# Second block: a fourth high-part buffer, tile 5 split before the first rotation, and a new order on ScalarE in the second attention

## Chip, cores and metric

The kernel runs on one core of a Trainium2 chip. The metric is the device time of one execution in microseconds; the median of three runs of the kernel before is 1157.89 us (1157.75 to 1158.03).

## What is computed

One sequence of 256 tokens with 1024 features passes through a first block of two layers (retention, forgetting attention and an RWKV-7 recurrence, gated and merged, then a gated feed-forward net) and a second block of two layers, with which this change deals. Cut to what matters, a layer of the second block is

```
h = rmsnorm(x, norm_g)                 # [256, 1024]
z = h @ w_in                           # 3328 columns: q,k,v,gate of branches a, b, c, d
q_a,k_a = axial_rope(rmsnorm(q_a)), axial_rope(rmsnorm(k_a)); o_a = softmax(q_a k_a^T / 8) v_a
q_b,k_b = rope(q_b), rope(k_b);        o_b = softmax with window and a sink logit
o_c = neighbourhood attention with a relative bias
o_d = (softmax(q1 k1^T) - lam * softmax(q2 k2^T)) v_d, rmsnorm
x = x + concat(o_a*silu(g_a), o_b*silu(g_b), o_c*silu(g_c), o_d*silu(g_d)) @ w_out
```

## The kernel before

Every large product is done in three passes of a float32 kind that TensorE takes fast: a weight tile is split into a high part (ScalarE, a copy that rounds) and a low part (VectorE, the tile minus the high part), and so is the activation.

In the second block the input projection goes over 13 groups of 256 columns. A group's weights are a tile of 1 MB, 128 x 2048. SyncE loads tile n into ring slot n % 4 once TensorE has finished group n - 3. ScalarE writes the high part (`in_split2` in its program, line 1373), VectorE the low part in place of the tile (`in_split2` in its program, line 1827). The high parts have three buffers in turn (`high2[l][n % 3]`), so ScalarE's helper `next_high(l, g)` waits for TensorE's group g before it splits tile g + 3. Tile 5 therefore waited for group 2. TensorE does a group in two units ("pieces", 12 matmuls of 512 columns each, line 669): pieces 2n and 2n + 1 belong to tile n, and a group's first piece waits for its tile's low part. Groups 0 to 11 come in pairs, which are copied out of PSUM by ScalarE together (`pair_out`, line 1652).

Every engine works its program in the written order; there is no planner. The order around the change is this, in each of the two layers.

TensorE: pieces 0 to 9 (tiles 0 to 4), with the norm's sum of squares in between; then the turn (transposes, line 1262) of q and k of branch a, which waits for the rotation; then piece 10, which waits for tile 5; then four attentions (`attend(n)`). In an attention the scores of heads 0 and 1 come first, a piece, the turn of the gate (`y_transposes`, line 754), a piece, then the wait for the gate's copy, `weigh(0)` (transposes of the probabilities, line 803), the scores of heads 2 and 3, `weigh(1)`, a piece, the values of a pair (line 826), `weigh(2)`, and so on. `weigh(h)` waits for the normalised probabilities of head h (VectorE, line 1897) and for the copy of the turned probabilities of head h - 1 (ScalarE's `copy`, line 1451).

VectorE: low parts of tiles 2, 3 and 4, the head sums of branch a, small products for lambda, then the wait for GpSimd's inverse roots (`b_rs`), the rotation (lines 2406, 2409, 1857, 1865, 1867), low parts of tiles 5 and 6, the gate product `(tanh + 1) * z` (line 2378), and the first attention. In an attention it makes for each head a mask addition (line 1909; none in the first) and a maximum, after each pair of heads the normalisation (`normed`), and splits of tiles at set places.

ScalarE: copy-outs, high parts, the tanh of a gate (`gate_sigmoid`, line 1670), and in the attentions the exponentials (`exps(n)`, line 1442), the copy of the turned gate (`gate_copy`, line 1428) and the copies of turned probabilities.

SyncE: the tile loads in order, line 551; between tile 4 and tile 5 its queue holds a wait for the norm's sum and the load of a small vector, and the load of the relative bias stands behind tile 7. GpSimd: the inverse roots (line 2488) and, when the relative bias has landed, two additions of it to the mask (line 2526).

Of the kernel before, what the change touches and what calls it, by code (L numbers as in the profile page):

```python
# [17 lines left out]
F32 = mybir.dt.float32  # L18
F32R = mybir.dt.float32r
ALU = mybir.AluOpType  # L20
ACT = mybir.ActivationFunctionType
AX = mybir.AxisListType

P = 128
D = 1024
KT = D // P
# [149 lines left out]
def build(nc, x_in, w_in, w_fox, lora_w, p_all, w_out, w_gate_up, w_down, cols, vec1, mu, w_in2, w_out2,  # L176
          vec2, rpb, tables, out):
    with ExitStack() as ctx:
        def sb(name, shape):
            return ctx.enter_context(nc.sbuf_tensor(name, shape, F32))  # L180
# [12 lines left out]
        ring = sb("ring", [P, RING, 2048])  # L193
        vec = sb("vec", [P, N_VEC1])
        yT_at = -(-nc.sbuf_base // 32) * 32
        yT = sb("yT", [P, 3, 2, S])
        lora = sb("lora", [P, 2, W4])
        w_f = sb("w_f", [P, KT, NH])
        w_f32 = sb("w_f32", [P, KT, 32])
        gain = sb("gain", [P, FINAL + 1, KT])  # L200
# [15 lines left out]
        def v2(n):  # L216
            return vec[:, VEC2[n][0]:VEC2[n][0] + VEC2[n][1]]
# [30 lines left out]
        in_high = [nc.alloc_sbuf_tensor_at(f"in_high{i}", [P, KT, 256], F32R, offset=ring_at + 8192 * (4 + i)) for i in range(2)]  # L248
        in_third = nc.alloc_sbuf_tensor_at("in_third", [P, KT, 256], F32R, offset=scratch_at + 4 * 2560)
        high2 = [(*in_high, in_third), (in_high[0], in_third, in_high[1])]  # L250
        in_low = [nc.alloc_sbuf_tensor_at(f"in_low{i}", [P, KT, 256], F32R, offset=ring_at + 8192 * i) for i in range(4)]

        wo_high = [nc.alloc_sbuf_tensor_at(f"out_high{q}", [P, 2, D], F32R, offset=o)
# [373 lines left out]
        def _(pe):  # L627
# [17 lines left out]

            def split_operands(n, l=None):

                return (in_high[n % 2] if l is None else high2[l][n % 3]), in_low[n % 4]

            def token_major(w, out, t):  # L650

# [693 lines left out]
        def _(act):  # L1345
# [24 lines left out]
            def in_split2(l, n):  # L1370

                act.wait_ge(*ring_in2[n % 4].after(l, n // 4 + 1))
                f(high2[l][n % 3][:], ring[:, n % 4, :].rearrange("p (k n) -> p k n", k=KT), ACT.Copy).then_inc(in_hi2.sem, 1)

            def in_split(l, n, slots, done):

# [271 lines left out]
            def pair_out(l, g):  # L1648

                act.wait_ge(*b_full.after(l, g + 2))  # L1650
                for t in range(NT):
                    last = f(z2[:, t, g * 256:(g + 2) * 256], bank[(g + t) % 4][:], ACT.Copy, scale=rstd_x[:, t:t + 1])
                last.then_inc(b_out.sem, 2)

            def next_high(l, g):

                act.wait_ge(*b_full.after(l, g + 1))
                in_split2(l, g + 3)
# [8 lines left out]
            def gate_sigmoid(l, c0):  # L1667

                e = b_eg_t.rearrange("p (t c) -> p t c", t=NT)
                f(e, z2[:, :, c0:c0 + W4], ACT.Tanh, scale=0.5).then_inc(b_eg.sem, 1)  # L1670

            qs = HD ** -0.5

            for l in range(DEPTH):
                in_split2(l, 2)
                next_high(l, 0)
                next_high(l, 1)
                sums(2 * DEPTH + l)
                act.wait_ge(*norms.root.after(2 * DEPTH + l, 1))
                pair_out(l, 0)  # L1680
                next_high(l, 2)
                act.wait_ge(*b_lam.after(l, 1))
                f(st[:, 200:202], st[:, 200:202], ACT.Exp).then_inc(b_lame.sem, 1)
                next_high(l, 3)
                pair_out(l, 2)
                next_high(l, 4)
                act.wait_ge(*b_out.after(l, 4))
                gate_sigmoid(l, 512)
                turned(l, 0, 256, qs)

                def gate_copy(n):
                    if n:
                        act.wait_ge(*b_mT.after(l, n))
                    y_copy(l, n, b_mtp, gT, bank[6], b_gT, 0.5)

                exps, copy = attention(l, att, 0, 0, 1, lambda n: bank[4 + n % 2])
                exps(0)
                exps(1)
                gate_copy(0)
                pair_out(l, 4)  # L1700
                next_high(l, 5)
                copy(0)
                copy(1)
                exps(2)
                exps(3)
                copy(2)
                next_high(l, 6)
                copy(3)
                turned(l, 2, 256, qs)
                pair_out(l, 6)  # L1710
                act.wait_ge(*b_out.after(l, 6))
                gate_sigmoid(l, 1280)

                exps, copy = attention(l, att, 4, 4, 1, lambda n: a_s[:, n % 2, :], sink=True)
                exps(0)
                exps(1)
                gate_copy(1)
                next_high(l, 7)
                copy(0)
                copy(1)  # L1720
                exps(2)
                exps(3)
                copy(2)
                next_high(l, 8)
                copy(3)
                turned(l, 4, 512, qs)
                pair_out(l, 8)
                next_high(l, 9)
                act.wait_ge(*b_out.after(l, 10))
                gate_sigmoid(l, 2304)  # L1730

                exps, copy = attention(l, att, 8, 8, 1, lambda n: a_s[:, n % 2, :])
                exps(0)
                exps(1)
                gate_copy(2)
                copy(0)
                copy(1)
                exps(2)
                exps(3)
                pair_out(l, 10)  # L1740
                copy(2)
                copy(3)
                turned(l, 6, 256, 32 ** -0.5)
                act.wait_ge(*b_full.after(l, G2))
                scaled(z2[:, :, (G2 - 1) * 256:G2 * 256], bank[(G2 - 1) % 4][:].rearrange("p (t c) -> p t c", t=2), rstd_x)\
                    .then_inc(b_out.sem, 1)
                fetch_x(l, x_saved2, x_back2)

                exps, copy = attention(l, att, 12, 12, 2, lambda n: bank[4 + n % 2])
                exps(0)  # L1750
                exps(1)
                exps(2)
                exps(3)
                copy(0)
                if l + 1 < DEPTH:
                    in_split2(l + 1, 0)
                exps(4)
                exps(5)
                copy(1)
                gate_sigmoid(l, 3072)  # L1760
                if l + 1 < DEPTH:
                    in_split2(l + 1, 1)
                exps(6)
                exps(7)
                copy(2)
                copy(3)
                act.wait_ge(*att.y.after(l, 4))
                f(b_t2, bank[7][:], ACT.Square).then_inc(b_lame.sem, 1)
                y_copy(l, 3, b_mtp, mixT[3], bank[7], b_mT, 0.5)
                if l + 1 < DEPTH:  # L1770
                    norm(2 * DEPTH + l + 1, fresh, x_saved2)
                else:

                    f(small[:, 9:10], eps6, ACT.Sqrt)
                    for j in range(4):
                        act.wait_ge(*x_ready.after(FINAL, j + 1))
                        f(squares[:, 2 * j:2 * j + 2, :], fresh[:, 2 * j:2 * j + 2, :], ACT.Square).then_inc(norms.sq.sem, 1)
                    act.wait_ge(*norms.summed.after(FINAL, 1))
                    f(root[:], bank[4][:, 0:S], ACT.Sqrt, scale=1.0 / D, bias=eps6).then_inc(norms.root.sem, 1)
# [3 lines left out]
        def _(dve):  # L1783
# [40 lines left out]
            def in_split2(l, n):  # L1824

                dve.wait_ge(*in_hi2.after(l, n + 1))
                tt(in_low[n % 4][:], ring[:, n % 4, :].rearrange("p (k n) -> p k n", k=KT), high2[l][n % 3][:].bitcast(F32),  # L1827
                   ALU.subtract).then_inc(in_lo2.sem, 1)

            def half_split2(l, n, half):  # L1830

                dve.wait_ge(*in_hi2.after(l, n + 1))
                k = slice(4 * half, 4 * half + 4)
                last = tt(in_low[n % 4][:, k, :], ring[:, n % 4, :].rearrange("p (k n) -> p k n", k=KT)[:, k, :],
                          high2[l][n % 3][:, k, :].bitcast(F32), ALU.subtract)
                if half:
                    last.then_inc(in_lo2.sem, 1)

# [527 lines left out]
            for l in range(DEPTH):  # L2366
# [35 lines left out]
                fence()  # L2402
                red(st[:, 200:202], st[:, 260:324].rearrange("p (a c) -> p a c", a=2), AX.X, ALU.add).then_inc(b_lam.sem, 1)
                ts(st[:, 330:394], v2("subln"), v2("one_less"), None, ALU.mult)
                dve.wait_ge(*b_rs.after(l, 1))
                tt(q_rot, qk6(0), put(st[:, 112:124].rearrange("p (t h) -> p t h", t=NT), 3, HD), ALU.mult)
                fence()
# [1 line left out]
                    tt(q_rot[:, :, h0:h1, :], q_rot[:, :, h0:h1, :], put(put(v2(n), 1, h1 - h0), 1, NT), ALU.mult)  # L2409
                fence()  # L2410
                rope(q_rot, q_t1, q_t2, q_rot, 6, "axial", 16).then_inc(b_rot.sem, 1)
                for n in range(5, 7):
                    in_split2(l, n)
                gate_ready(l, 1, 512)
                attention(l, att, 0, 4, 1, None, splits={1: lambda l: in_split2(l, 7)})

# [191 lines left out]
```

## Time and profile before

| | us |
|---|---|
| median of three runs | 1157.89 |
| the profiled execution's own time | 1157.58 |
| its span | 1155.5 |
| TensorE busy | 1126.9 |
| VectorE busy | 767.5 |
| ScalarE busy | 524.1 |

The second block covers the span from about 863 us on; layer 1 of it begins at about 1003. TensorE's granted clock is full (1.00) in all of it but the last microseconds. Times in rows are from the span's start. Engines are named PE (TensorE), PEld (its weight loads), DVE (VectorE), ACT (ScalarE), POOL (GpSimd), SPq (SyncE's DMA queue). A row of a timeline has the start, the duration, the engine, the line, the operation, what it writes and reads, the count of merged instructions, and in brackets how long the engine stood idle before it and which instruction ended that.

### The profile page before, as it was taken

To read this page: it belongs to the slowest core of one execution; us is meant where nothing else is said; L and a number is where in the kernel's file an instruction comes from. 1 tells how busy PE (TensorE), PEld (TensorE's weight loads), DVE (VectorE), ACT (ScalarE), POOL (GpSimd) and SP (SyncE) were. 2 spreads that over 40 slices of the span, in tenths; PEclk is the share of its full clock that TensorE was granted. 3 is DMA by queue.
4 is the path that set the end of the run, shared out by engine and by line. 5 is a ranking of instruction groups with operands and counts; after the bars stand their busy time and mean duration, and the time that the engine had idled before them with its cause. 6 is when DMAs were issued, how large, how long until landed. Compare 5 with 4: busy or idle time off the path is not lost. (4 is left out here: it accounts for less than half of the span.)

```text
span 1155.5 us, 21951 instructions
## 1 busy us (share of the span) xinstructions
PE 1126.9 (98%) x9400; PEld 1013.9 (88%) x9400; DVE 767.5 (66%) x1104; ACT 524.1 (45%) x734; POOL 65.7 (6%) x51
## 2 busy tenths in 40 slices
PE   5999999999999999999999999999999999999997
PEld 4789989899999998798998999999997768877785
DVE  5587765867565665787665965556667685677744
ACT  5355443534333344465334443333355565446642
POOL 1002000100000000011001000000001100030000
PEclk9999999999999999999999999999999999999999
DMA  9543335445354355443335355534436234353320
GB/s 358 222 163 110 116 109 188 176 164 224 159 218 187 144 199 187 146 146 111 111 111 220 109 219 219 216 140 189 181 141 229 109 111 182 115 218 134 116 79 37
DMA packets 27610, 188.16 MB, mean 163 GB/s; under 512 B 3472, under 2 KB 4368, under 8 KB 5776
## 3 DMA queue, kind: packets, MB, share of 16 engines
q1 hardware_dynamic: 25952, 175.89, 40.7%
q10 hardware_dynamic: 1440, 8.55, 1.9%
q0 software_dynamic: 144, 2.66, 0.6%
q8 instruction: 56, 0.92, 0.3%
q14 instruction: 18, 0.15, 0.0%
HBM read 181.84 MB, written 5.24 MB: 162 GB/s over the span
## 5 line engine op out<-in xcount | busy, mean ns | idle before, releaser
L669 PE MATMUL bank<-in_low,h_high 128*128 128x512 f32 x352 | 138.3, 393 | 0.0
L669 PE MATMUL bank<-in_high,h_high 128*128 128x512 f32 x288 | 117.5, 408 | 12.5 <-DVE in_low L1977 11.8
L1089 PE MATMUL bank<-h_high,gate_split 128*128 128x256 f32 x704 | 128.8, 280 | 0.2
L1089 PE MATMUL bank<-h_high,up_split 128*128 128x256 f32 x704 | 128.6, 280 | 0.0
L1105 PE MATMUL bank<-act_split,down_split 128*128 128x256 f32 x960 | 118.4, 283 | 0.0
L1105 PEld LDWEIGHTS bank<-act_split,down_split 128*128 128x128 f32 x960 | 116.6, 192 | 0.0
L694 PE MATMUL bank<-h_high,in_high 128*128 128x256 f32 x384 | 115.8, 302 | 0.5 <-DVE in_low L1851 0.5
L1378 ACT ACTIVATE in_high<-ring 128x2048 fp32r<-128x2048 f32 x47 | 89.6, 1910 | 54.9 <-PE bank L669 53.6
L669 PE MATMUL bank<-in_high,x_low 128*128 128x512 f32 x288 | 113.1, 393 | 0.0
L1089 PEld LDWEIGHTS bank<-h_high,gate_split 128*128 128x128 f32 x704 | 109.9, 189 | 0.9 <-DVE h_low L1793 0.6
L1089 PEld LDWEIGHTS bank<-h_high,up_split 128*128 128x128 f32 x704 | 109.8, 189 | 0.0
L694 PE MATMUL bank<-x_low,in_high 128*128 128x256 f32 x384 | 108.4, 282 | 0.0
L694 PE MATMUL bank<-h_high,in_low 128*128 128x256 f32 x384 | 108.3, 282 | 0.0
L1851 DVE TENSOR_TENSOR in_low<-ring,in_high 128x2048 fp32r<-128x2048 f32 x35 | 79.9, 2289 | 35.4 <-ACT in_high L1378 35.4
L1089 PE MATMUL bank<-h_low,up_split 128*128 128x256 f32 x352 | 99.2, 282 | 0.0
L1089 PE MATMUL bank<-h_low,gate_split 128*128 128x256 f32 x352 | 99.1, 282 | 0.0
L1609 ACT ACTIVATE gate_split<-ring 128x2048 fp32r<-128x2048 f32 x24 | 46.0, 1916 | 73.2 <-PE bank L1089 71.5
L2290 DVE TENSOR_TENSOR down_split<-ring,down_split 128x2048 fp32r<-128x2048 f32 x20 | 45.9, 2292 | 50.0 <-ACT down_split L1609 50.0
L669 PEld LDWEIGHTS bank<-in_low,h_high 128*128 128x128 f32 x352 | 66.7, 189 | 13.2 <-issue 0.5
L694 PEld LDWEIGHTS bank<-h_high,in_high 128*128 128x128 f32 x384 | 73.1, 190 | 5.7 <-issue 1.4
L669 PEld LDWEIGHTS bank<-in_high,h_high 128*128 128x128 f32 x288 | 54.5, 189 | 26.3 <-issue 14.3
L694 PEld LDWEIGHTS bank<-x_low,in_high 128*128 128x128 f32 x384 | 73.4, 191 | 0.1
(348 smaller groups left out, 2385.2 us busy)
## 6 DMA issues: line engine op xcount, KB each, us to landing
ring<-w_in_dram SPq DMA_DIRECT2D x71, 1024.0 KB, 4.9
ring<-w_gate_up_dram SPq DMA_DIRECT2D x44, 1024.0 KB, 8.3
ring<-w_down_dram SPq DMA_DIRECT2D x22, 1024.0 KB, 4.8
ring<-w_out_dram SPq DMA_DIRECT2D x16, 1024.0 KB, 6.5
ring<-p_all_dram SPq DMA_DIRECT2D x6, 1024.0 KB, 4.8
x_kept<-scratch ACTq DMA_DIRECT2D x4, 1024.0 KB, 3.9
x<-x_kept ACTq DMA_DIRECT2D x4, 1024.0 KB, 8.4
table<-tables_dram POOLq DMA_DIRECT2D x1, 2594.0 KB, 11.9
```

Source lines behind the costliest of these rows:

```text
L669: last = mm(bank[(n - n % 2 + t) % 4][:], a, b, start=c == 0 and i == 0, stop=c == KT - 1 and i == 2)
L694: last = mm(bank[g % 4][:, half * 256:(half + 1) * 256], a, b, start=k == 0 and i == 0, stop=k == KT - 1 and i == 2)
L1089: last = mm(bank[2 * half + part][:, f * S:(f + 1) * S], a, b, start=k == 0 and i == 0, stop=k == KT - 1 and i == 2)
L1105: last = mm(bank[4 + m // 2][:, m % 2 * S:(m % 2 + 1) * S], a, b, start=False, stop=end and m % 2 == 1 and k == 1 and i == 2)
L1378: f(in_high[n % 2][:], ring[:, n % 4, :].rearrange("p (k n) -> p k n", k=KT), ACT.Copy).then_inc(done.sem, 1)
L1609: f(w_split[part if pair is None else pair][:, 0, :], ring[:, 3 * half + part, :], ACT.Copy).then_inc(w_hi[part].sem, 1)
L1851: tt(in_low[n % 4][:], ring[:, n % 4, :].rearrange("p (k n) -> p k n", k=KT), in_high[n % 2][:].bitcast(F32), ALU.subtract).then_inc(low.s ...
L2290: tt(w[:, 1, :], ring[:, 3 * half + part, :], w[:, 0, :].bitcast(F32), ALU.subtract)\
```

## The change

A tensor of 512 columns is laid behind `lora`, so that there is room for a fourth high-part buffer, over parts of `yT` and `lora` that the second block does not use and that new tensor. Tile 5 of each layer goes into it. ScalarE splits tile 5 without a wait for group 2. VectorE makes the low part of tile 5 before the wait for the inverse roots and the rotation, and no longer behind it. In front of the second attention ScalarE does the second gate's tanh ahead of the copy-out of groups 6 and 7; in it, the gate's copy comes between the first two exponentials, and the split of tile 10 comes behind the first two copies of turned probabilities.

```
         lora = sb("lora", [P, 2, W4])
+        sb("after_lora", [P, 512])
...
+        in_fourth = nc.alloc_sbuf_tensor_at("in_fourth", [P, KT, 256], F32R, offset=yT_at + 4 * 512)
+
+        def high_of(l, n):
+            return in_fourth if n == 5 else high2[l][n % 3]
...
-                return (in_high[n % 2] if l is None else high2[l][n % 3]), in_low[n % 4]
+                return (in_high[n % 2] if l is None else high_of(l, n)), in_low[n % 4]
...
                 pair_out(l, 0)
-                next_high(l, 2)
+                in_split2(l, 5)
                 act.wait_ge(*b_lam.after(l, 1))
...
                 turned(l, 2, 256, qs)
-                pair_out(l, 6)
                 act.wait_ge(*b_out.after(l, 6))
                 gate_sigmoid(l, 1280)
+                pair_out(l, 6)
 
                 exps, copy = attention(l, att, 4, 4, 1, lambda n: a_s[:, n % 2, :], sink=True)
                 exps(0)
+                gate_copy(1)
                 exps(1)
-                gate_copy(1)
-                next_high(l, 7)
                 copy(0)
                 copy(1)
+                next_high(l, 7)
                 exps(2)
...
                 ts(st[:, 330:394], v2("subln"), v2("one_less"), None, ALU.mult)
+                in_split2(l, 5)
                 dve.wait_ge(*b_rs.after(l, 1))
...
                 rope(q_rot, q_t1, q_t2, q_rot, 6, "axial", 16).then_inc(b_rot.sem, 1)
-                for n in range(5, 7):
-                    in_split2(l, n)
+                in_split2(l, 6)
                 gate_ready(l, 1, 512)
```

The other hunks write `high_of(l, n)` for `high2[l][n % 3]` in the splits of both engines.

## Rows read from the trace of the kernel before

**Rows 1.** The page's part 1: busy time, share of the span, instructions.
```profile
PE 1126.9 (98%) x9400; PEld 1013.9 (88%) x9400; DVE 767.5 (66%) x1104; ACT 524.1 (45%) x734; POOL 65.7 (6%) x51
```

**Rows 2.** TensorE's waits, 860 to 1156 us: total, times, longest.
```profile
PE bank L669 <- DVE in_low L1827: 1.6, 2, 0.9
PE bank L803 <- ACT scratch L1451: 1.3, 2, 0.7
PE bank L803 <- ACT scratch L1428: 0.9, 2, 0.5
...
```

**Rows 3.** Timeline of TensorE at the first turn, both layers.
```profile
891.15 0.82 PE L1262 MATMUL bank<-table,scratch 128*128 128x128 f32 x6
892.89 0.50 PE L669 MATMUL bank<-in_third,h_high 128*128 128x512 f32 x1 [0.92 <-DVE in_low L1827]
...
1032.15 0.82 PE L1262 MATMUL bank<-table,scratch 128*128 128x128 f32 x6
1033.67 0.49 PE L669 MATMUL bank<-in_high,h_high 128*128 128x512 f32 x1 [0.71 <-DVE in_low L1827]
```

**Rows 4.** Timeline of ScalarE: the high part of tile 5, both layers.
```profile
884.81 1.92 ACT L1373 ACTIVATE in_third<-ring 128x2048 fp32r<-128x2048 f32 x1 [4.24 <-DMA ring<-w_in_dram]
...
1025.53 1.92 ACT L1373 ACTIVATE in_high<-ring 128x2048 fp32r<-128x2048 f32 x1 [4.18 <-DMA ring<-w_in_dram]
```

**Rows 5.** Timeline of SyncE's queue: loads of tiles 5 to 7, layer 0.
```profile
877.89 8.34 SPq L551 DMA_DIRECT2D ring<-w_in_dram  x3
```

**Rows 6.** Timeline of VectorE: the first rotation and what follows, both layers.
```profile
885.43 0.96 DVE L2406 TENSOR_TENSOR scratch<-arena,small 128x768 f32<-128x768 f32 x1 [2.25 <-POOL small L2488]
...
889.68 0.96 DVE L1867 TENSOR_TENSOR scratch<-scratch 128x768 f32<-128x768 f32 x1
890.55 2.29 DVE L1827 TENSOR_TENSOR in_low<-ring,in_third 128x2048 fp32r<-128x2048 f32 x1
892.76 2.28 DVE L1827 TENSOR_TENSOR in_low<-ring,in_high 128x2048 fp32r<-128x2048 f32 x1
894.96 2.87 DVE L2378 SCALAR_TENSOR_TENSOR scratch<-scratch,arena 128x512 f32<-128x512 f32 x1
...
1026.21 0.96 DVE L2406 TENSOR_TENSOR scratch<-arena,small 128x768 f32<-128x768 f32 x1 [2.25 <-POOL small L2488]
```

**Rows 7.** Timeline of GpSimd: the first bias addition, both layers.
```profile
893.15 4.13 POOL L2526 TENSOR_TENSOR scratch<-scratch,table 128x1024 f32<-128x1024 f32 x1 [7.75 <-DMA scratch<-rpb_dram]
...
1033.95 4.11 POOL L2526 TENSOR_TENSOR scratch<-scratch,table 128x1024 f32<-128x1024 f32 x1 [7.78 <-DMA scratch<-rpb_dram]
```

**Rows 8.** Timeline of VectorE in the second attention, layer 0.
```profile
919.46 0.69 DVE L2378 SCALAR_TENSOR_TENSOR scratch<-scratch,arena 128x512 f32<-128x512 f32 x1 [4.08 <-ACT scratch L1670]
...
931.37 0.15 DVE L1891 TENSOR_TENSOR stats<-stats,small 128x2 f32<-128x2 f32 x1
```

**Rows 9.** Timeline of TensorE in the second attention, layer 0.
```profile
917.53 1.13 PE L787 MATMUL bank<-scratch 64*128 64x256 f32 x8
...
921.50 0.60 PE L754 MATMUL bank<-table,scratch 128*128 128x128 f32 x4
...
925.34 0.66 PE L803 MATMUL bank<-table,scratch 128*128 128x128 f32 x4 [0.45 <-ACT scratch L1428]
...
927.71 0.63 PE L803 MATMUL bank<-table,scratch 128*128 128x128 f32 x4 [0.65 <-ACT scratch L1451]
...
932.51 0.66 PE L803 MATMUL bank<-table,scratch 128*128 128x128 f32 x4 [0.27 <-DVE scratch L1897]
```

**Rows 10.** Timeline of ScalarE in the second attention, layer 0.
```profile
921.86 0.51 ACT L1442 ACTIVATE scratch<-scratch,stats 128x256 f32<-128x256 f32 x1 [2.43 <-DVE stats L1923]
...
924.71 0.57 ACT L1428 ACTIVATE scratch<-bank 128x512 f32<-128x512 f32 x1
925.19 1.90 ACT L1373 ACTIVATE in_high<-ring 128x2048 fp32r<-128x2048 f32 x1
```

**Rows 11.** Windows: busy us of each engine, PEclk (granted clock), DMA share, GB/s.
```profile
1152.00:1156.00 4.00, 0.00 (x0) 0.00 (x0) 0.52 (x1) 0.00 (x0) 0.00 (x0) 0.50 0.64 255
```

More of the change, by code:

```diff
@@ L197, in build @@
         lora = sb("lora", [P, 2, W4])
+        sb("after_lora", [P, 512])
         w_f = sb("w_f", [P, KT, NH])
@@ L250, in build, with high_of @@
         high2 = [(*in_high, in_third), (in_high[0], in_third, in_high[1])]
+        in_fourth = nc.alloc_sbuf_tensor_at("in_fourth", [P, KT, 256], F32R, offset=yT_at + 4 * 512)
+        def high_of(l, n):
+            return in_fourth if n == 5 else high2[l][n % 3]
         in_low = [nc.alloc_sbuf_tensor_at(f"in_low{i}", [P, KT, 256], F32R, offset=ring_at + 8192 * i) for i in range(4)]
@@ L646, in split_operands @@
             def split_operands(n, l=None):
-                return (in_high[n % 2] if l is None else high2[l][n % 3]), in_low[n % 4]
+                return (in_high[n % 2] if l is None else high_of(l, n)), in_low[n % 4]
             def token_major(w, out, t):
@@ L1372, in in_split2 @@
                 act.wait_ge(*ring_in2[n % 4].after(l, n // 4 + 1))
-                f(high2[l][n % 3][:], ring[:, n % 4, :].rearrange("p (k n) -> p k n", k=KT), ACT.Copy).then_inc(in_hi2.sem, 1)
+                f(high_of(l, n)[:], ring[:, n % 4, :].rearrange("p (k n) -> p k n", k=KT), ACT.Copy).then_inc(in_hi2.sem, 1)
             def in_split(l, n, slots, done):
@@ L1680, in _ @@
                 pair_out(l, 0)
-                next_high(l, 2)
+                in_split2(l, 5)
                 act.wait_ge(*b_lam.after(l, 1))
@@ L1709, in _ @@
                 turned(l, 2, 256, qs)
-                pair_out(l, 6)
                 act.wait_ge(*b_out.after(l, 6))
                 gate_sigmoid(l, 1280)
+                pair_out(l, 6)
                 exps, copy = attention(l, att, 4, 4, 1, lambda n: a_s[:, n % 2, :], sink=True)
                 exps(0)
+                gate_copy(1)
                 exps(1)
-                gate_copy(1)
-                next_high(l, 7)
                 copy(0)
                 copy(1)
+                next_high(l, 7)
                 exps(2)
@@ L1826, in in_split2 @@
                 dve.wait_ge(*in_hi2.after(l, n + 1))
-                tt(in_low[n % 4][:], ring[:, n % 4, :].rearrange("p (k n) -> p k n", k=KT), high2[l][n % 3][:].bitcast(F32),
+                tt(in_low[n % 4][:], ring[:, n % 4, :].rearrange("p (k n) -> p k n", k=KT), high_of(l, n)[:].bitcast(F32),
                    ALU.subtract).then_inc(in_lo2.sem, 1)
@@ L1834, in half_split2 @@
                 last = tt(in_low[n % 4][:, k, :], ring[:, n % 4, :].rearrange("p (k n) -> p k n", k=KT)[:, k, :],
-                          high2[l][n % 3][:, k, :].bitcast(F32), ALU.subtract)
+                          high_of(l, n)[:, k, :].bitcast(F32), ALU.subtract)
                 if half:
@@ L2404, in _ @@
                 ts(st[:, 330:394], v2("subln"), v2("one_less"), None, ALU.mult)
+                in_split2(l, 5)
                 dve.wait_ge(*b_rs.after(l, 1))
@@ L2411, in _ @@
                 rope(q_rot, q_t1, q_t2, q_rot, 6, "axial", 16).then_inc(b_rot.sem, 1)
-                for n in range(5, 7):
-                    in_split2(l, n)
+                in_split2(l, 6)
                 gate_ready(l, 1, 512)
```

## The prediction

> **What bounds the kernel now.** I read four things, in this order. The page's first lines say that TensorE is busy for 98% of the span, so only two things can move the end: TensorE work, which this change does not touch, and TensorE's waits [rows 1]. The list of TensorE's waits in the second block comes next; it shows short kinds only, the longest 0.9 us, each once per layer; three of them are what the edits touch [rows 2]: the wait for the low part of tile 5 behind the first rotation, and the two waits in the second attention that ScalarE ends. Third, TensorE's own timeline at these places; fourth, that of the engines which feed them. What counts there is not how long TensorE waits now but which engine would be last after the move. A wait reads a little short in its bracket, since matmul ends are modelled and the next instruction normally starts before the recorded end. I therefore compare starts. Where nothing waits, an instruction follows 0.06 to 0.16 us before the recorded end of the one ahead (1.13 us of scores from 917.53, the next unit at 918.60 by the timeline), so that a turn of six transposes (0.82) is followed after some 0.75 and eight score matmuls (1.13) after 1.07 [rows 3, 9].
>
> **Edit 1, the fourth buffer and ScalarE's earlier split of tile 5.** The old line waited for group 2 on TensorE, the new one waits only for the tile's load. But ScalarE's wait of 4.24 us before this split was ended by the DMA, not by TensorE: the load is issued at 877.89 and the split starts when it has landed, at 884.81; in layer 1 the wait is 4.18 us, again for the DMA [rows 4, 5]. The load's issue is not changed: SyncE holds it behind the wait for the norm's sum and the small vector load, both ahead of it in its queue. So the high part of tile 5 is ready at 884.81 + 1.92 = 886.73, exactly as before. The edit is worth 0. The dummy tensor of 512 columns costs no time.
>
> **Edit 2, the low part of tile 5 ahead of the rotation on VectorE.** Before, VectorE sat 2.25 us waiting for GpSimd's inverse roots and began the rotation at 885.43; its last instruction (line 1867) started at 889.68, 4.25 us after the first, and took 0.96; then came the low part of tile 5 (2.29), that of tile 6 (2.28) and the gate product [rows 6]. TensorE's turn began at 891.15 without a wait, and the unit behind it (piece 10) at 892.89, where it would have begun at 891.90 had tile 5 been there: the stall is 0.99 us. Layer 1: the unit began at 1033.67, and 1032.15 + 0.75 = 1032.90 would have been possible, so 0.77 [rows 3].
> After the move VectorE reaches the split at about 883.2 and waits for the high part. It starts it at 886.76 (0.03 after ScalarE's end, an estimate from the hand-over 1027.45 to about 1027.48), the next instruction 2.20 later (as 890.55 is followed by 892.76), so the rotation starts at 888.97 and not at 885.43. That is 3.54 us late. Nothing covers it: the turn on TensorE waits for the rotation, and everything behind the turn is queued in order. Rotation end: 888.97 + 4.25 + 0.96 = 894.18; turn at 894.22; piece 10 at 894.97 and not 892.89: **+2.08 us** in layer 0. In layer 1: high part ready 1025.53 + 1.92 = 1027.45, rotation 1029.68 to 1034.89, turn 1034.94, piece 10 1035.69 against 1033.67: **+2.02 us** [rows 3, 4, 6]. The stall that the edit means to remove is gone, a stall of 3 us ahead of the turn takes its place.
>
> **Edit 2 has a second price.** GpSimd's first bias addition starts at 893.15 when its DMA lands, and takes 4.13 us; the second takes 2.8. The gate product on VectorE, 0.69 us elsewhere, took 2.87 us beside them [rows 6, 7]. Read together: the addition stood until tile 6's low part ended (895.04) and then ran about 2.24; the gate product stood until the addition ended (897.28) and then took 0.55. Two instructions of these engines that both read SBUF run one after the other, and the earlier one goes first. Before the change the rotation was over by then. Now its last addition starts at 888.97 + 4.25 = 893.22, GpSimd's at 893.15. In layer 1 it is 1033.93 against 1033.95 [rows 6, 7]. By these rows GpSimd is first in layer 0 by 0.07 us and VectorE first in layer 1 by 0.02. Who comes second waits: if it is VectorE, for 893.15 + 2.34 = 895.49, and the rotation ends some 0.82 later, at 896.31 and not 894.18: another **2.1 us** on TensorE's path (2.34 is an estimate: 2.24 plus about 0.1 of start). If it is GpSimd, VectorE's split of tile 6 stands behind the bias addition, which tile 6 bears, as it is wanted only two units later. I take one collision out of two. Bounds of this term: 0 and 4.3 us.
> The Trainium skill, page "SBUF — State Buffer", section "Who interferes with whom", says the same of a VectorE instruction with two SBUF inputs against a GpSimd instruction that reads SBUF: whichever issues first holds the shared pair for the whole instruction. By that rule the trace agrees (2.87 for 0.69), and the rule speaks against moving the rotation to where the bias addition lands.
>
> **Edit 3, the gate's tanh ahead of the copy-out of groups 6 and 7.** Before, ScalarE waited 3.38 us for TensorE's group 7, copied out until 918.90, and then did the tanh; VectorE waited 4.08 us for it and started its gate product at 919.46, the first mask 0.61 later at 920.07 [rows 8]. With the tanh first (groups 4 and 5 are long copied out), the gate product is done beside TensorE's last projection unit. The mask then waits for the scores, which start at 917.53 and can be read 1.2 us later: 918.73 [rows 9]. That moves the softmax chain up by 1.34 us; exps(0), which began at 921.86, runs 920.52 to 921.80 [rows 10].
>
> **Edit 4, the gate copy ahead of exps(1), the split of tile 10 behind the copies.** The gate copy is now limited by TensorE's turn of the gate, 921.50 to 922.10: it runs 922.14 to 922.72 and not at 924.71 [rows 9, 10]. TensorE's weigh(0) starts at 924.74 and not 925.34 (stall 0.60 gone), the scores at 925.27, weigh(1) 1.07 later at 926.34, since copy(0) at 925.38 to 925.98 no longer stands behind 1.9 us of splitting (before: 927.71, 0.72 of it stall) [rows 9]. What is late next is weigh(2), which waits for the normalised third head. exps(1) starts behind the gate copy at 922.63 and ends at 923.91 (before 924.80); VectorE normalises from 923.94, so its split of tile 9, masks and maxima move up by 0.90, and normed(2) would be possible at 931.37 - 0.90 = 930.47 [rows 8]. But ScalarE now has the split of tile 10 (1.90, before at 925.19) between copy(1) (ends 927.58) and exps(2): 927.48 to 929.39, exps(2) 929.30 to 930.58 where its maximum was ready at 928.94. normed(2) starts at 930.61, weigh(2) 1.14 later (as 931.37 to 932.51 before) at 931.75. TensorE is there 1.02 us earlier: the third stall grows from 0.34 to 1.0. **Net gain 932.51 - 931.75 = 0.76 us**, the same in layer 1 (0.78, the same rows 140.8 us later) [rows 8 to 10]. Tiles 10 and 11 follow earlier by as much and have over 1.5 us in hand. Bounds: 0.3 (VectorE's unexplained gap of 0.46 us before a scaling falls into this chain) and 1.32 (both stalls go and nothing grows).
>
> **Sum.** On the profiled execution of 1157.58 us (span 1155.5 and 2.1 around it): 1157.58 + 2.08 + 2.02 + 2.1 - 0.76 - 0.78 = 1162.2. The median of the runs is 0.3 above the profiled one, so 1162.6 for the timing. Nothing later gives the delay back: behind the turn TensorE has no wait in the first attention that could shrink, and loads and splits follow TensorE's groups.
>
> **Rivals.**
> *No collision.* VectorE's rotation goes first in both layers: 1157.9 + 4.1 - 1.54 = 1160.4. For it: the margins are 0.07 and 0.02 us. Chance 0.26.
> *Collision in both layers:* 1160.4 + 4.3 = 1164.7, since layer 1's order hangs on 0.02 us. With it TensorE idles from 891.3 to 896.4. TensorE's last matmul of all is over before 1148, and from 1152 the granted clock stands at 0.50 [rows 11], the lower level (1.2 GHz): some 4 us of idleness had gone before. An idle stretch of 5 us may bring that too, and a unit of 3.05 us at half clock costs up to 3 us more; a stretch of 2.9 us (no collision) is shorter than that one. Chance 0.24.
> The Trainium skill, page "TensorE: Matmul & The Clock Gate", section "Part 1: The HAM clock gate", has the clock go down after an idle stretch; by it the two-collision case would reach some 1167, and the trace agrees that idleness lowers it.
> *Faster.* The fourth buffer lets the split of tile 5 run in the idle time. It would if the tile landed by 881: high part 880.6 to 882.5, low part inside VectorE's 2.25 us wait for GpSimd, rotation not late, and 0.99 + 0.77 + 1.54 = 3.3 us won: 1154.6. It decides at the landing, and the rows have it at 884.8 with the issue untouched. Chance 0.06.
> *No change in the end.* The moved split costs only what the second attention brings, for instance because VectorE's drains between the rotation's parts shorten: within 1.5 us, 1158 to 1159. No row speaks for it. Chance 0.06.
>
> **The numbers.** One collision has 0.38, and 1162.6. The range leaves out the faster case, most of no change and the clock's full price: 1160.2 to 1165.8. 0.2% is 2.3 us, about what a measurement of this kernel can tell from no change, so slower begins at 1160.2: nearly all of three cases, less 0.08 of the first rival that falls under it. Faster 0.06, same 0.14, slower 0.80.
>
> **What would show it.** In the changed kernel: ScalarE's split of tile 5 still ends a wait of about 4.2 us on the DMA; VectorE's low part of tile 5 at about 886.8 and the rotation from 889.0; TensorE waiting about 2.9 us (or 5) before the turn at line 1262 in both layers, and none before piece 10; a rotation addition of 3 us in place of 0.96 where it met the bias addition; the two ScalarE waits in the second attention gone and the one on line 1897 near 0.7 to 1.0. I am wrong if tile 5's high part comes before 884, or if the turn starts near 891.2.

## The result, and the profile after

The changed kernel takes 1165.59 us in the median of six runs (1163.64 to 1169.43), the kernel before 1157.69 on the same occasions (1157.42 to 1158.03): ratio 1.0071, 95% interval 1.0056 to 1.0087. It is slower by 7.9 us where 4.7 were forecast. The kernel before scatters by 0.6 us, the changed one by 5.8. The profiled execution took 1165.16 us, its span is 1163.0 against 1155.5: 7.5 us more. Line numbers of the changed kernel are 6 higher (line 669 is 675, 1867 is 1873).

TensorE's waits in the second block, total, times and longest:

```profile
PE bank L1268 <- DVE scratch L1873: 7.7, 2, 5.1
...
PE bank L809 <- DVE scratch L1903: 0.7, 2, 0.4
PE bank L675 <- DVE in_low L1833: 0.7, 2, 0.4
```

Beside [rows 2], the two waits that ScalarE ended are gone, and a wait for the rotation (line 1873) stands ahead of the turn in both layers. The timelines of ScalarE and VectorE at the first rotation, layer 0, then layer 1; they answer to [rows 4] and [rows 6]:

```profile
884.96 1.92 ACT L1379 ACTIVATE in_fourth<-ring 128x2048 fp32r<-128x2048 f32 x1 [4.46 <-DMA ring<-w_in_dram]
...
1030.36 1.92 ACT L1379 ACTIVATE in_fourth<-ring 128x2048 fp32r<-128x2048 f32 x1 [4.12 <-DMA ring<-w_in_dram]
```

```profile
886.91 2.29 DVE L1833 TENSOR_TENSOR in_low<-ring,in_fourth 128x2048 fp32r<-128x2048 f32 x1 [3.77 <-ACT in_fourth L1379]
889.12 0.95 DVE L2413 TENSOR_TENSOR scratch<-arena,small 128x768 f32<-128x768 f32 x1
...
893.36 2.95 DVE L1873 TENSOR_TENSOR scratch<-scratch 128x768 f32<-128x768 f32 x1
896.23 4.45 DVE L1833 TENSOR_TENSOR in_low<-ring,in_high 128x2048 fp32r<-128x2048 f32 x1
...
1034.52 0.95 DVE L2413 TENSOR_TENSOR scratch<-arena,small 128x768 f32<-128x768 f32 x1
...
1038.76 0.96 DVE L1873 TENSOR_TENSOR scratch<-scratch 128x768 f32<-128x768 f32 x1
1039.63 4.46 DVE L1833 TENSOR_TENSOR in_low<-ring,in_high 128x2048 fp32r<-128x2048 f32 x1
```

GpSimd's bias additions, as [rows 7] (the first row holds both of layer 0, the second the first of layer 1):

```profile
893.09 5.44 POOL L2532 TENSOR_TENSOR scratch<-scratch,table 128x1024 f32<-128x1024 f32 x2 [7.77 <-DMA scratch<-rpb_dram]
...
1039.34 2.60 POOL L2532 TENSOR_TENSOR scratch<-scratch,table 128x1024 f32<-128x1024 f32 x1 [8.28 <-DMA scratch<-rpb_dram]
```

The high part of tile 5 still waits for the DMA. The rotation starts at 889.12, 3.7 us later than before. In layer 0 the bias addition came 0.27 us ahead of the rotation's last addition, which took 2.95 us and not 0.96. In layer 1 the rotation went first (0.96), and the split of tile 6 paid (4.46 for 2.29). That is the forecast's case of one collision. TensorE at the turn, as [rows 3], and the granted clock (third column from the right) at these places:

```profile
896.36 1.39 PE L1268 MATMUL bank<-table,scratch 128*128 128x128 f32 x6 [5.14 <-DVE scratch L1873]
897.40 0.78 PE L675 MATMUL bank<-in_fourth,h_high 128*128 128x512 f32 x1
...
901.53 1.14 PE L793 MATMUL bank<-scratch 64*128 64x256 f32 x8
...
1039.77 1.43 PE L1268 MATMUL bank<-table,scratch 128*128 128x128 f32 x6 [2.58 <-DVE scratch L1873]
1040.86 0.78 PE L675 MATMUL bank<-in_fourth,h_high 128*128 128x512 f32 x1
...
1044.95 1.14 PE L793 MATMUL bank<-scratch 64*128 64x256 f32 x8
```

```profile
894.00:896.00 2.00, 0.00 (x0) 0.00 (x0) 2.00 (x1) 0.00 (x0) 2.00 (x2) 1.00 0.65 270
896.00:898.00 2.00, 1.64 (x8) 1.54 (x9) 2.00 (x2) 0.64 (x2) 2.00 (x1) 0.64 0.00 0
898.00:900.00 2.00, 2.00 (x6) 1.61 (x5) 2.00 (x1) 0.23 (x1) 0.53 (x1) 0.50 0.00 0
900.00:902.00 2.00, 2.00 (x11) 1.39 (x12) 1.28 (x2) 0.00 (x0) 0.00 (x0) 1.00 0.00 0
...
1038.00:1040.00 2.00, 0.23 (x2) 0.23 (x3) 1.93 (x5) 1.66 (x2) 0.66 (x1) 0.98 0.93 303
1040.00:1042.00 2.00, 2.00 (x9) 1.81 (x8) 2.00 (x1) 0.87 (x2) 2.00 (x2) 0.50 0.63 262
1042.00:1044.00 2.00, 2.00 (x8) 1.59 (x7) 2.00 (x1) 0.00 (x0) 2.00 (x1) 0.66 0.00 0
```

The turn in layer 0 began at 896.36, where the forecast had it for a collision. But the granted clock fell to 0.50, the lower level (1.2 GHz), and stayed there for some 3.4 us: the turn took 1.39 us and not 0.82, its unit reached the scores 4.1 us after its start and not 3.0. In narrow windows the fall stands not in the idle stretch but 0.2 us behind the start of the turn (1.00 up to 896.4, 0.93 in the mean of 896.4 to 896.6, 0.50 from there). The same happened in layer 1, after an idle stretch of only 2.6 us (1.00 up to 1039.8, 0.83 in 1039.8 to 1040).

The second attention, TensorE, layer 0, beside [rows 9]:

```profile
923.15 1.13 PE L793 MATMUL bank<-scratch 64*128 64x256 f32 x8
...
932.96 0.50 PE L675 MATMUL bank<-in_high,h_high 128*128 128x512 f32 x1 [0.36 <-DVE in_low L1833]
...
937.38 0.66 PE L809 MATMUL bank<-table,scratch 128*128 128x128 f32 x4 [0.36 <-DVE scratch L1903]
```

From the scores to weigh(2) it is 14.23 us, before 932.51 - 917.53 = 14.98: 0.75 won. In layer 1 it is 14.19 against 14.98 (1073.28 - 1058.30): 0.79.

Where the 7.5 us are, by the start of the scores of the first attention (before: 895.90 and 1036.63): layer 0 901.53 - 895.90 = +5.63, then -0.75, and layer 1 begins 4.89 late; 1044.95 - 1036.63 = 8.32, of which layer 1 adds 3.43, then -0.79. Sum 7.52.

### The profile page after: what moved, and what is told of

It reads as the page before. It is cut to its first block, busy times and chain, and to the rows that moved or that the text cites. A ratio compares the mean times of both kernels' runs of the same rounds, so it can differ in the third digit from the quotient of the medians.

```text
span 1163.0 us, 21949 instructions
## 1 busy us (share of the span) xinstructions
PE 1130.2 (97%) x9400; PEld 1016.8 (87%) x9400; DVE 771.6 (66%) x1104; ACT 524.3 (45%) x734; POOL 64.2 (6%) x51
## 4 chain that ended last, share of the span: by engine, by line
PE 82%; DVE 10%; ACT 4%; DMA 2%; DVEq 1%; issue 1%; POOL 1%; POOLq 0%; SPq 0%; ACTq 0%
PE bank L1095 21%; PE bank L675 16%; PE bank L1111 11%; PE bank L700 10%; PE bank L1075 4%; PE bank L1057 4%; PE bank L793 2%; PE bank L1245 2%; DVE in_low L1857 2%; PE bank L1239 1%; PE bank L809 1%; DMA ring<-w_in_dram 1%; PE bank L832 1%; PE bank L661 1%; DVE in_low L1833 1%
## 5 line engine op out<-in xcount | busy, mean ns | idle before, releaser
L675 PE MATMUL bank<-in_high,h_high 128*128 128x512 f32 x280 | 114.3, 408 | 12.2 <-DVE in_low L1983 11.5
L675 PE MATMUL bank<-in_high,x_low 128*128 128x512 f32 x280 | 110.1, 393 | 0.0
```

The source lines that it names most:

```text
L675: last = mm(bank[(n - n % 2 + t) % 4][:], a, b, start=c == 0 and i == 0, stop=c == KT - 1 and i == 2)
```

## Experiments

**The moved split undone.**

```
                 ts(st[:, 330:394], v2("subln"), v2("one_less"), None, ALU.mult)
-                in_split2(l, 5)
...
-                in_split2(l, 6)
+                for n in range(5, 7):
+                    in_split2(l, n)
```

> The changed kernel with the low part of tile 5 back behind the rotation on VectorE; the fourth buffer, ScalarE's earlier split and its new order in the second attention stay. Theory (all of the loss hangs on the moved split: rotation late, then collision with the bias addition, then TensorE's clock): the loss goes and the gain of the second attention stays, 1157.7 - 0.75 - 0.79 = 1156.1 us. Rival (the fourth buffer's place, over yT and lora, or the missing wait for group 2 makes TensorE or ScalarE slower): part of the 7.9 us stays, over 1158.

Measured 1156.47 us (1155.96 to 1156.87, 10 runs; before 1157.93), ratio 0.9987, interval 0.9977 to 0.9996. All of the loss hangs on VectorE's moved split; the rest of the change gains 1.5 us. The rival on the buffer's place falls.

**The moved split alone**, in the kernel before (the reverse of that diff, three buffers):

> The kernel before with only VectorE's split of tile 5 moved ahead of the rotation, three buffers and ScalarE's old order. Theory: the whole loss without the attention's gain, 1165.6 + 1.5 = 1167.1 us, with the same scatter of some us from run to run. Rival (the buffer matters): under 1163.

Measured 1168.09 us (1167.05 to 1169.35, 4 runs), ratio 1.0090 (1.0073 to 1.0107). The trace has the same waits of 5.1 and 2.6 us ahead of the turn, and the clock at 0.50 in both turns. In layer 0, though, it fell at 893.9, in the midst of the idle stretch and 2.2 us behind TensorE's last matmul (which ended at 891.7), and came back only at 900.7, after some 7 us:

```profile
892.00:894.00 2.00, 0.00 (x0) 0.00 (x0) 1.93 (x6) 2.00 (x2) 0.39 (x1) 0.97 0.94 328
894.00:896.00 2.00, 0.00 (x0) 0.00 (x0) 2.00 (x1) 0.17 (x1) 2.00 (x2) 0.50 0.90 377
...
900.00:902.00 2.00, 2.00 (x9) 1.47 (x7) 1.75 (x2) 0.00 (x0) 0.00 (x0) 0.82 0.00 0
```

VectorE's last rotation addition and GpSimd's bias addition, layer 0:

```profile
893.67 3.10 DVE L1867 TENSOR_TENSOR scratch<-scratch 128x768 f32<-128x768 f32 x1
```

```profile
893.61 5.38 POOL L2526 TENSOR_TENSOR scratch<-scratch,table 128x1024 f32<-128x1024 f32 x2 [7.80 <-DMA scratch<-rpb_dram]
```

GpSimd was ahead by 0.06 us, and that decided 2.1 us. In layer 1 VectorE was ahead by 0.14 (1040.23 to 1040.37) and took 0.96.

**The bias additions behind the rotation**, in the changed kernel, so that they can't collide:

```
                 pool.wait_ge(*rpb_in.after(l, 1))
+                pool.wait_ge(*b_rot.after(l, 1))
```

> The changed kernel with GpSimd's bias additions made to wait for the rotation. Theory (collision in layer 0 worth 2.2 us, clock worth 1.4 us in each layer): rotation's last addition 0.96 in both layers, wait ahead of the turn 2.6 to 2.9 us in both, clock still falls in most executions; 1157.7 + 4.1 + up to 2.9 - 1.5 = 1160.3 to 1163.2. Rival (the surplus over the forecast came from collisions in both layers, not from the clock): 1160.3, and no stretch at half clock.

Measured 1164.39 us (1161.93 to 1165.39, 4 runs), ratio 1.0057 (1.0041 to 1.0074). The profiled execution is the one of 1161.93. Its turns:

```profile
894.58 0.87 PE L1268 MATMUL bank<-table,scratch 128*128 128x128 f32 x6 [3.05 <-DVE scratch L1873]
...
1036.81 1.54 PE L1268 MATMUL bank<-table,scratch 128*128 128x128 f32 x6 [2.98 <-DVE scratch L1873]
```

No collision in either layer. After 3.05 us of idleness the clock was still full in layer 0, after 2.98 us it had fallen in layer 1 (0.79 in the mean of 1034 to 1038, 0.78 of 1038 to 1042): the same idleness, one with and one without the fall. The rival of two collisions falls. But the other three executions, at 1163.8 to 1165.4, lie up to 2.2 us above what both falls explain at 1.4 us each, and they have no trace. Their mean granted clocks are known: 0.997 for the profiled execution, 0.996 for the one of 1163.83, 0.994 for 1164.96, 0.993 for 1165.39; the slower, the lower. From 0.997 to 0.993 is, by estimate, 9 us more at the lower level (0.004 of 1163 us, doubled), where the profiled execution had one stretch of 3.4 us. So the clock can carry the surplus as well, by longer stretches such as the one of 7 us above. That is not shown: what of it fell into work, and what into idleness, where it costs nothing, no trace tells, and in the four executions of the moved split alone the order is the other way (1167.05 at 0.993, 1169.35 at 0.995).

**TensorE kept at work in that wait**, as the last one and

```
+                for i in range(12):
+                    mm(bank[6][:], zeros[:], h_high[:, 0:2, :].rearrange("p k s -> p (k s)"), start=True, stop=True)
                 turn(l, 0, rotated, b_rot, 1)
```

> As e3_bias_late, and TensorE does 12 matmuls of 512 columns on zeros into an unused bank in the time in which it waits for the rotation. Theory (clock): no half clock any more, the turn of six transposes takes 0.82 and not 1.4, its unit 3.05 and not 4.2; 1160.3 us, with little scatter. Rival (the slower turn and unit come from something else, such as cold weights or the buffer): turn and unit stay slow, time as e3_bias_late or above.

Measured 1160.28 us (1159.40 to 1160.95, 10 runs), ratio 1.0019 (1.0009 to 1.0029). Layer 1:

```profile
1034.10 2.92 PE L1286 MATMUL bank<-h_high,zeros 128*128 128x512 f32 x12
1036.86 0.86 PE L1268 MATMUL bank<-table,scratch 128*128 128x128 f32 x6
...
1040.43 1.14 PE L793 MATMUL bank<-scratch 64*128 64x256 f32 x8
```

Twelve matmuls a layer whose result nobody uses made it 4.1 us faster than the kernel without them. The clock is at 1.00 up to the kernel's last microseconds, the turn takes 0.86, and the time is the one that the prediction's sum gives for no collision, 1160.4. That shows the clock to be what the sum lacks.

**Tile 5 loaded earlier.** In the changed kernel SyncE's vector load stands behind tile 5 and not behind tile 4:

```
-                    if n == 4:
+                    if n == 5:
 
                         sp.wait_ge(*norms.summed.after(2 * DEPTH + l, 1))
                         sp.dma_start(vec[:, 0:N_VEC2], ...)
```

> The changed kernel with one line of SyncE's queue changed: the load of tile 5 is issued ahead of the wait for the norm's sum and the small vector load, no longer behind them. Theory (the moved split is late only because tile 5 lands at 884.9): tile 5 lands by 880, its high part is done by 882.5, its low part fits in VectorE's wait for the inverse roots, rotation and turn begin when they did before the change, no stall at either; 1157.9 - 0.99 - 0.77 - 1.54 = 1154.6 us. Rival (the earlier load collides with the weight loads around it or delays the small vector, and the rotation is late anyway): 1157 or more.

Measured 1157.51 us (1157.04 to 1157.95, 10 runs), ratio 0.9999 (0.9989 to 1.0008). That is the rival's number, but not for its reason: the tile came in time, and the turn still waited 1.49 and 1.26 us. ScalarE, VectorE, GpSimd, TensorE:

```profile
881.28 1.93 ACT L1379 ACTIVATE in_fourth<-ring 128x2048 fp32r<-128x2048 f32 x1
```

```profile
883.91 2.28 DVE L1833 TENSOR_TENSOR in_low<-ring,in_fourth 128x2048 fp32r<-128x2048 f32 x1
888.35 0.96 DVE L2413 TENSOR_TENSOR scratch<-arena,small 128x768 f32<-128x768 f32 x1 [2.16 <-POOL small L2494]
```

```profile
883.95 4.37 POOL L2494 TENSOR_TENSOR small<-small,table 128x12 f32<-128x12 f32 x1
```

```profile
893.62 0.87 PE L1268 MATMUL bank<-table,scratch 128*128 128x128 f32 x6 [1.49 <-DVE scratch L1873]
```

The split was meant to use VectorE's wait for GpSimd's inverse roots. It starts 0.04 us ahead of the power instruction that makes them, which then takes 4.37 us, 2.27 without it (883.13 to 885.40 in the kernel before), and VectorE waits for it another 2.16 us. What was to hide in the wait held up the very instruction that the wait is for: the collision again, the other way round.

**The same with three buffers** (`high2[l][n % 3]` and `next_high(l, 2)` back):

> As e5_early_load, but tile 5's high part in the third of three buffers, with ScalarE's wait for group 2. Theory (the fourth buffer gives nothing, since group 2 ends before ScalarE comes to the split): the same as e5_early_load within 0.3 us. Rival (the fourth buffer is what an early load needs): slower than e5_early_load by over 1 us.

Measured 1157.21 us (1156.87 to 1157.82, 10 runs), 0.3 below the last one: the fourth buffer gives nothing.

**Only the load**, in the kernel before:

> The kernel before with only the load of tile 5 issued earlier. Theory (VectorE's order, low part behind the rotation, makes the stall at piece 10): no change, 1157.9 us. Rival (the landing alone was the limit): 1156.1.

Measured 1157.99 us (1157.44 to 1158.37), ratio 1.0000 (0.9990 to 1.0009): as expected.

**The load and the moved split, ScalarE's old order:**

> The kernel before with the earlier load of tile 5 and VectorE's moved split; three buffers, ScalarE's old order in the second attention. Theory: only the stall at piece 10 goes, 1157.9 - 1.76 = 1156.1 us, and the two ScalarE waits in the second attention stay. Rival (edits help each other, the gains don't add): over 1157 or under 1155.5.

Measured 1159.00 us (1158.71 to 1159.26), ratio 1.0010 (1.0000 to 1.0020). The number was missed, for the same waits ahead of the turn (2.8 us in both layers together); the difference to the kernel with the new order, 1.5 us, is again the second attention's gain, so the gains do add.

**A memset ahead of the split**, to let the power instruction go first:

```
+                nc.vector.memset(kept[:, 0:256], 0.0)
                 in_split2(l, 5)
```

> As e5_early_load, with one small memset (256 columns of a tensor that this block does not use) on VectorE ahead of the low part of tile 5. In e5_early_load VectorE's split started at 883.91, 0.04 us before GpSimd's power instruction, which then took 4.37 us and not 2.27. Theory (the two stand in each other's way, and the one that starts first goes first; a power instruction already running does not hold up a split, as at 480.3 us of the kernel before): with the split some 0.2 us later the power takes 2.3 us again, the rotation starts by 886.6 on that clock, the wait before the turn goes in both layers, 1157.9 - 1.76 - 1.54 = 1154.6 us. Rival (it is the overlap as such that slows GpSimd, or VectorE's split is then the one held up): power near 4.4 us or split over 4 us, 1157.5.

Measured 1157.96 us (1157.48 to 1158.41, 11 runs), ratio 0.9999 (0.9990 to 1.0008): missed, the rival's number came. **The same with three buffers:**

> As e9_behind_root, with three high-part buffers and ScalarE's wait for group 2 as before the change. Theory (the fourth buffer gives nothing): as e9_behind_root within 0.3 us. Rival: slower by over 0.5 us.

Measured 1157.98 us (1157.30 to 1158.54). Again no difference by the buffer. The first one's VectorE and GpSimd:

```profile
883.64 0.27 DVE L2411 MEMSET kept<- 128x256 f32 x1
883.83 2.23 DVE L1833 TENSOR_TENSOR in_low<-ring,in_fourth 128x2048 fp32r<-128x2048 f32 x1
```

```profile
883.59 4.58 POOL L2495 TENSOR_TENSOR small<-small,table 128x12 f32<-128x12 f32 x1
```

The power started 0.24 us ahead of the split and was held up all the same. Either it needs longer to take hold, or the memset stood in its way. The last two kernels tell these apart, with a reduction in the memset's place.

```
+                red(stats[:, 112:120].rearrange("p (t h) -> p t h", t=NT), q_t1[:, :, 0:4, :], AX.X, ALU.add)
                 in_split2(l, 5)
```

> As e5_early_load, with a reduction of 512 columns into unused columns (about 0.7 us, one input) ahead of the low part of tile 5 on VectorE. Theory (a power instruction wants VectorE to be off two-input work only in its first fraction of a microsecond; 0.24 us was too short in e9_behind_root, 0.65 us was enough at 480.3 us of the kernel before): the power takes 2.3 us, the rotation starts at the end of the split, about 0.6 us behind its old time, the wait before the turn is 0.2 to 0.5 us per layer; about 1155.5 us. Rival (the power instruction of 12 columns is held up by a split at any time): power over 4 us, 1157.5 or more.

> The same with a reduction of 128 columns (about 0.25 us, as long as the memset of e9_behind_root). If the memset itself stood in GpSimd's way, the power takes 2.3 us here; if the power's start takes over 0.25 us to reach the point where it is safe, it takes over 4 us as in e9_behind_root.

The long reduction: 1154.56 us (1154.17 to 1155.23, 7 runs; before 1157.76), ratio 0.9972, interval 0.9960 to 0.9983. The short one, one run: 1154.31. VectorE and GpSimd with the short one:

```profile
883.23 0.28 DVE L2411 TENSOR_REDUCE stats<-scratch 128x2 f32<-128x128 f32 x1
883.42 2.28 DVE L1833 TENSOR_TENSOR in_low<-ring,in_fourth 128x2048 fp32r<-128x2048 f32 x1
```

```profile
883.27 2.27 POOL L2495 TENSOR_TENSOR small<-small,table 128x12 f32<-128x12 f32 x1
```

The split now starts only 0.15 us behind the power, and the power takes 2.27. So the power does not need longer to take hold, and the rival that a split holds it up at any time falls. What held it up with the memset is narrowed down, not settled: the memset started 0.05 us behind the power, both reductions 0.03 to 0.04 us ahead of it, so that the kind of instruction and the order of the starts changed together; no run has a memset ahead of the power or a reduction behind it. With the power let through, the wait ahead of the turn is gone from the list of waits in both kernels; of the 0.2 to 0.5 us that were expected to remain nothing did, and 1154.56 is 0.9 below the 1155.5 expected. The one with the long reduction is faster than both the kernel before (by 3.2 us) and the changed one.

## Why the prediction was wrong

- *Edit 1 is worth 0*: right. The high part still waited for the DMA (4.46 and 4.12 us), and two pairs of kernels with three and four buffers differ by 0.3 and 0.02 us. In the kernels with the reductions, the fastest, three buffers were not tried.
- *The moved split makes the rotation late, +2.08 and +2.02 us*: right. The kernel with neither collision nor fallen clock takes 1160.28 us, the forecast for it was 1160.4.
- *One collision of two, +2.1 us in layer 0*: right, in the profiled execution: 2.95 for 0.96, the turn at the very 896.36 that its working gives (896.31 and the hand-over). That the count came out is in part luck: the order hung on 0.07 us in the forecast and was 0.27 in the trace; in layer 1 it hung on 0.02 and was 0.58 (1038.76 against 1039.34), the bias landing later there. Its general sentence, that two instructions of these engines that both read SBUF run one after the other, goes too far: with the short reduction GpSimd's power (883.27, 2.27 us) and VectorE's split (883.42, 2.28 us) ran side by side and neither was held up.
- *TensorE's clock*: this step failed. The sum had no term for it, and the text let it come only in the case of two collisions, because "a stretch of 2.9 us (no collision) is shorter than that one". By the prediction's own working the stretch of 5 us, from 891.3 to 896.3, stands in layer 0 of the one-collision case too, so that even by its own reading the likeliest case should have had the clock's price once. The runs show the fall behind idle stretches of 5.1, 3.0 and 2.6 us, and once not behind 3.05. Against the forecast's terms it costs 5.63 - 4.18 = 1.45 us in layer 0 and 3.43 - 2.02 = 1.41 in layer 1: together the 2.9 us that the sum lacks in the profiled execution (7.5 against 4.6). Row against row it is 1.6 us each: from the turn to the scores 5.17 and 5.18 us here, 3.58 and 3.57 in the kernel with the twelve matmuls. The forecast had 0.75 + 3.01 = 3.76 for that piece of work, 0.2 too much, which hid as much of the clock's price. One row of the kernel before, an idle stretch of some 4 us that ended with the clock low, was read as a lower bound; it was one case. The price was bounded ("up to 3 us"), but it was left out of the likeliest sum and its range.
- *The second attention, -0.76 and -0.78 us*: right, 0.75 and 0.79. On the way one wait of 0.36 us that had not been named came, for the low part of tile 9 ahead of its unit. It cost nothing, as weigh(2) behind it is set by VectorE; it only took its 0.36 us from the third wait, which reads 0.36 in its bracket and not 0.7 to 1.0.
- *The rival "faster"* put the whole decision at the tile's landing. With the landing moved, the gain did not come (1157.51): its low part, said to fit "inside VectorE's 2.25 us wait for GpSimd", held up what VectorE was waiting for. The forecast had read this very collision in [rows 6, 7] for the bias addition and did not apply it to the inverse roots. With that mended the rival's number, 1154.6, is met: 1154.56. An early landing alone did not suffice.
- The scatter of the changed kernel, 5.8 us, was expected from the thin margin of the collisions; the fall of the clock, present in one of two equal waits, adds to it. The slowest run (1169.43) also has the lowest mean granted clock, 0.993 where the other five have 0.994 to 0.995 and the kernel before 0.998. But the moved split alone has its lowest clock, 0.993, in its fastest run, so that the mean clock decides nothing by itself: how much of the slowest run is clock and how much a second collision is open, there being no trace of it.

## What to carry to other kernels

When a change puts an idle stretch of some microseconds into a TensorE that was always busy, price the clock with it, behind each stretch, as a chance and not as nothing; twelve matmuls on zeros in each of the two stretches were worth 4 us together here. Before filling an engine's wait, ask what the engine that it waits for is doing and whether the filler takes something from it: here a split that started 0.04 us ahead of GpSimd's power nearly doubled it (4.37 us for 2.27), and one that started 0.15 us behind it cost nothing. And ask of a load's landing, not of a buffer, whether an earlier step can start.

## What the runs showed of the hardware that was not expected

- Between VectorE and GpSimd, a start 0.04 or 0.06 us earlier decided over 2.1 us: GpSimd's addition ahead by 0.06 held up VectorE's (3.10 for 0.96), VectorE's split ahead by 0.04 held up GpSimd's power (4.37 for 2.27). The other way round the power held up nothing: started 0.15 us ahead of a split, it took 2.27 and the split 2.28.
- With a memset of 256 float32 columns on VectorE started 0.04 to 0.06 us behind GpSimd's power and the split behind that, the power took 4.58 and 4.59 us, in both layers of both kernels with the memset, and ended 2.1 us behind the split's end. With a reduction of the same length in its place, started 0.03 to 0.04 us ahead of the power, it took 2.27. The Trainium skill, page "SBUF — State Buffer", section "Who interferes with whom", lets only VectorE instructions with two SBUF inputs or in a two-port mode contend; a memset reads nothing. Here the measurement differs for this one form, if the memset and not the order of the starts made the difference, and unless this memset ran in such a mode, which no trace here shows.
- TensorE's granted clock was at 0.50 behind idle stretches of 5.1, 3.0 and 2.6 us and at 1.00 behind one of 3.05 us. Of two stretches of 5.1 us, one saw it fall 2.2 us after the last matmul and stay low for some 7 us, the other only after the turn had begun, for 3.4 us. From the turn to the scores a fall cost 1.3 to 1.8 us.
